# Hybrid decoder step on one core: page numbers read ahead, a logits buffer for each prompt tile, output weights in two places, unread products in two pauses

## The reference

```python
def layer_step(x, pos, lp, attn, ...):
    cols = x @ lp['w_in']
    ...                                   # rotary, indexer keys
    y_a = attn(q, k, v, qi, ki, wi)       # top-k attention, 4 heads of 64
    y_b, ... = rwkv7_mix(...)             # recurrence with a matrix state
    y_c, ... = gated_short_conv(...)
    y_d, ... = rglru_block(...)
    mix = jnp.concatenate([y_a, y_b, y_c, y_d], axis=-1) @ lp['w_out']
    x = layer_norm(DEEPNORM_ALPHA * x + mix, lp['ln1_g'], lp['ln1_b'])
    ffn = moe(x, w_router, router_bias, ...)      # 16 experts, 2 for each row
    x = layer_norm(DEEPNORM_ALPHA * x + ffn, lp['ln2_g'], lp['ln2_b'])

# in attention, for the keys selected by the indexer
logits = jnp.einsum('bthd,btkhd->bthk', q, k_sel) * A_HEAD_DIM ** -0.5
logits = jnp.where(valid[:, :, None, :], logits, -jnp.inf)
p = jax.nn.softmax(logits, axis=-1)
return jnp.einsum('bthk,btkhd->bthd', p, v_sel)
```

## Time and profile before

| | us |
|---|---|
| median of 3 runs (1496.24 to 1502.35) | 1501.76 |
| profiled execution | 1498.81 |
| its span | 1497.2 |
| TensorE busy in the span | 1235.8 |
| VectorE / ScalarE / GpSimd busy | 662.0 / 345.4 / 160.3 |

### The profile page before, as it was taken

How to read it: one execution, slowest core, us unless ns; L and a number is a source line. 1 busy time by engine, 2 the same in 40 slices (tenths; PEclk the granted TensorE clock), 3 DMA queues, 4 the chain that set the end, 5 groups by cost and what they waited for, 6 DMA issues and landing times.

```text
span 1497.2 us, 22283 instructions
## 1 busy us (share of the span) xinstructions
PE 1235.8 (83%) x8296; PEld 777.7 (52%) x8296; DVE 662.0 (44%) x1379; ACT 345.4 (23%) x798; POOL 160.3 (11%) x224
## 2 busy tenths in 40 slices
PE   4989999985899099999398899998679944999950
PEld 2566778952445044444156677897344532444420
DVE  0036898876144301111453469997632350111118
ACT  1044241204222011111143423320322210111110
POOL 0040007003000200000201000430310002000011
PEclk9988999986799599999699799998789966999985
DMA  6095210016442469997512021100538005999943
GB/s 255 7 380 231 71 57 19 4 49 183 182 198 94 180 237 365 355 368 264 192 69 64 15 70 57 42 8 3 150 115 345 1 28 218 332 367 368 358 152 128
DMA packets 67917, 246.30 MB, mean 165 GB/s; under 512 B 8722, under 2 KB 29362, under 8 KB 58674
## 3 DMA queue, kind: packets, MB, share of 16 engines
q1 hardware_dynamic: 48736, 177.17, 32.9%
q0 software_dynamic: 14048, 50.00, 9.4%
q10 hardware_dynamic: 5042, 17.90, 2.9%
HBM read 194.39 MB, written 52.87 MB: 165 GB/s over the span
## 4 chain that ended last, share of the span: by engine, by line
PE 73%; DVE 10%; ACT 4%; DMA 3%; issue 3%; SPq 3%; DVEq 2%; POOL 1%; POOLq 0%; ACTq 0%
PE ps L1227 15%; PE ps L694 12%; PE ps L827 10%; PE ps L1245 8%; PE ps L1190 8%; PE ps L674 7%; PE ps L1218 2%; SPq L446 1%; PE ps L753 1%; PE ps L1062 1%; DMA arena<-in_wa 1%; POOL rows_in L613 1%; ACT arena L1298 1%; SPq L443 1%; DVE arena L1840 1%
## 5 line engine op out<-in xcount | busy, mean ns | idle before, releaser
L1298 ACT ACTIVATE arena<-ps 128x512 f32<-128x512 f32 (+14 forms) x358 | 155.5, 470 | 693.8 <-PE ps L694 155.5
L694 PE MATMUL ps<-arena 128*128 128x272 f32 x1088 | 261.1, 400 | 0.0
L694 PEld LDWEIGHTS ps<-arena 128*128 128x128 f32 x1088 | 208.9, 193 | 50.6 <-issue 5.5
L1227 PE MATMUL ps<-arena 128*128 128x512 f32 x512 | 230.1, 602 | 4.8 <-ACT arena L1298 4.8
L1227 PEld LDWEIGHTS ps<-arena 128*128 128x128 f32 x512 | 98.3, 193 | 130.1 <-issue 130.1
L827 PE MATMUL ps<-arena 64*64 64x64 f32 (+3 forms) x4016 | 153.1, 236 | 12.5 <-DVE arena L2057 10.3
L827 PEld LDWEIGHTS ps<-arena 64*64 64x64 f32 x4016 | 138.5, 137 | 26.3 <-issue 14.7
L674 PE MATMUL ps<-arena 128*128 128x512 f32 (+1 forms) x256 | 105.6, 573 | 22.5 <-DMA arena<-in_wa 19.0
L1245 PE MATMUL ps<-arena 128*128 128x512 f32 x256 | 117.7, 602 | 3.8 <-DVE arena L2513 3.8
L1190 PE MATMUL ps<-arena 128*128 128x512 f32 x256 | 114.1, 601 | 0.0
L2513 DVE COPY arena<-ps 128x256 f32<-128x256 f32 x32 | 13.6, 426 | 188.1 <-PE ps L1234 188.1
(11 more groups left out here) (344 smaller groups left out, 1322.5 us busy)
## 6 DMA issues: line engine op xcount, KB each, us to landing
arena<-in_w_gu SPq DMA_DIRECT2D x32, 2048.0 KB, 9.9
arena<-in_w_dn SPq DMA_DIRECT2D x32, 1024.0 KB, 9.2
arena<-in_wf SPq DMA_DIRECT2D x34, 512.0 KB, 3.7
arena<-rows_in SPq DMA_DIRECT2D x32, 512.0 KB, 9.6
rows_out<-arena ACTq DMA_DIRECT2D x32, 512.0 KB, 8.4
rows_in<-arena POOLq DMA_DIRECT2D x12, 1024.0 KB, 24.2
arena<-in_cache_v POOLq DMA_DIRECT2D x64, 128.0 KB, 2.7
arena<-in_cache_k SPq DMA_DIRECT2D x64, 128.0 KB, 2.7
```

The lines of the kernel that those rows point to most:

```text
L694: mm = pe.matmul(ps[:, 2 + 2 * h + n % 2, 0:HALF], m.wf[n % 3][:, c, :], m.xT[:, c, h * HALF:h * HALF + HALF], start=c == 0, stop=c == KC - 1)
L1227: mm = pe.matmul(ps[:, 3 + k, :], m.xgT[:, c, :], m.w_gu[k][:, c, :], start=c == 0, stop=c == KC - 1)
L1298: return act.activation(out, in_, ACT.Copy)
```

## The change

Five things are edited.

1. The page numbers are read into 32 registers on SyncE and on GpSimd ahead of the wait for the recurrence; the loops over the pages are written out.
2. `m.lg` gets four buffers, one for each tile, two of them in LN0; the maxima and sums get four places too. The wait on `pt_mm` in `masked` goes. The lists of TensorE, ScalarE and VectorE are put in another order: logits(2) ahead of output(0), logits(3) ahead of output(1), the sample's logits ahead of output(2); three maskings before the first scaling; the sample's exponentials ahead of tile 3's copies.
3. The output weights are loaded in two halves, into R2 (after the sample's first logits half) and R1 (after tile 2's values). Expert 0's weights, which also lie in R2, are loaded after the projection's last product instead of at the end of attention.
4. The scatters of tiles 0 to 2 and of tiles 3 and 4 are counted in two semaphores.
5. `warm(n)` puts n products of 128x512 into a PSUM bank that nobody reads: 6 after the first of these semaphores, 5 after the first gathered rows of layer 0's last norm.

```diff
-    m.lg, m.pT = [view(R1, 4, 384), view(R1 + 4096, 4, PAST)], [view(R1 + 6144, 4, 384), view(R1 + 1536, 4, PAST)]
+    m.lg = [view(at, 4, P * (i + 1)) for i, at in enumerate((LN0 + DM, LN0, R1, R1 + 4096))]
+    m.pT = [view(R1 + 1536, 4, 384), view(R1 + 6144, 4, PAST)]
...
+        def page_of(b):
+            return sp.value_load(pages[0:1, b:b + 1], min_val=0, max_val=NPHYS - 1)
+
+        ahead = [page_of(b) for b in range(32)]
         sp.wait_ge(s["rw_mm"], nth(l, "rw_mm", len(RW_PE)))
...
-        for g in range(2):
-            with sp.Fori(0, 4) as j:
-                for c in range(NPAGE):
-                    page = sp.value_load(pages[0:1, bass.ds(j * NPAGE + (16 * g + c), 1)], min_val=0, max_val=NPHYS - 1)
-                    if g and c == 0:
-                        sp.wait_ge(s["state_out"], nth(l, "state_out", 64))
-                    sp.dma_start(m.K[g][:, :, bass.ds(j, 1), PAGE * c:PAGE * c + PAGE],
...
-        sp.wait_ge(s["pv_mm"], nth(l, "pv_mm", 4))
-        sp.dma_start(m.wout, layer_of(din["wout"], l)).then_inc(s["wout_in"], 16)
+        for b in range(2 * 4 * NPAGE):
+            g, j, c = b // (4 * NPAGE), b // NPAGE % 4, b % NPAGE
+            page = ahead[b] if b < len(ahead) else page_of(b)
+            if b == 4 * NPAGE:
+                sp.wait_ge(s["state_out"], nth(l, "state_out", 64))
+            sp.dma_start(m.K[g][:, :, j:j + 1, PAGE * c:PAGE * c + PAGE],
...
+        sp.wait_ge(s["s_lg_mm"], nth(l, "s_lg_mm", 1))
+        sp.dma_start(m.wout[0], layer_of(din["wout"], l)[:, 0:KC // 2, :]).then_inc(s["wout_in"], 16)
+        sp.wait_ge(s["pv_mm"], nth(l, "pv_mm", 3))
+        sp.dma_start(m.wout[1], layer_of(din["wout"], l)[:, KC // 2:KC, :]).then_inc(s["wout_in"], 16)
...
-        for k in range(2):
-            up_weights(k, k)
-            down_weights(k, k)
+        up_weights(1, 1)
+        down_weights(1, 1)
+        sp.wait_ge(s["mix_mm"], nth(l, "mix_mm", 5))
+        up_weights(0, 0)
+        down_weights(0, 0)
...
-        sp.wait_ge(s["x_scattered"], nth(l, "x_scattered", 160))
+        sp.wait_ge(s["x_scattered"], nth(l, "x_scattered", 96))
+        sp.wait_ge(s["x_spread"], nth(l, "x_spread", 64))
...
+    def warm(n):
+
+        for _ in range(n):
+            pe.matmul(ps[:, 7, :], ident, m.consts[:, 0:512], start=True, stop=True)
...
+        pe.wait_ge(s["yg0_in"], nth(l - 1, "yg0_in", 32))
+        warm(5)
         transposes_of_x(l - 1, 5, 0, 0)
...
         y_gates(l, (6, 6), slice(SEQ, T))
+        logits(2)
         pe.wait_ge(s["yn_std"], nth(l, "yn_std", 1))
         output(0)
-        logits(2)
+        logits(3)
         output(1)
-        logits(3)
+        sample_logits(l)
         output(2)
-        sample_logits(l)
         output(3)
...
         mm.then_inc(s["slots_mm"], 1)
+        pe.wait_ge(s["x_scattered"], nth(l, "x_scattered", 96))
+        warm(6)
...
         y_norm(l)
-        exps(0)
-        for i in range(NT):
-            if i + 1 < NT:
-                exps(i + 1)
-            else:
-                for g in range(2):
-                    act.wait_ge(s["s_lg_mm"], nth(l, "s_lg_mm", g + 1))
-                    copy(m.s_lg[g][:, 0:PAST], ps[:, 2 - 2 * g, :])
-                    copy(m.s_lg[g][:, PAST:T], ps[:, 3 - 2 * g, 0:NS]).then_inc(s["s_lg"], 1)
-            turned(i)
-            output(i)
-
+        for i in range(3):
+            exps(i)
+        turned(0)
+        output(0)
+        turned(1)
+        output(1)
+        exps(3)
+        for g in range(2):
+            act.wait_ge(s["s_lg_mm"], nth(l, "s_lg_mm", g + 1))
+            copy(m.s_lg[g][:, 0:PAST], ps[:, 2 - 2 * g, :])
+            copy(m.s_lg[g][:, PAST:T], ps[:, 3 - 2 * g, 0:NS]).then_inc(s["s_lg"], 1)
+        turned(2)
+        output(2)
         for g in range(2):
             act.wait_ge(s["s_max"], nth(l, "s_max", g + 1))
             act.activation(m.s_lg[g], m.s_lg[g], ACT.Exp, bias=m.nmax[g][:, 0:1], accum_out=m.ssum[g][:, 0:1])\
                 .then_inc(s["s_exp"], 1)
+        turned(3)
+        output(3)
...
             dve.wait_ge(s["lg_mm"], nth(l, "lg_mm", i + 1))
-            if i >= 2:
-                dve.wait_ge(s["pt_mm"], nth(l, "pt_mm", 4 * (i - 1)))
...
         y_centred(l)
-        masked(0)
-        masked(1)
-        normed(0)
+        for i in range(3):
+            masked(i)
+        for i in range(3):
+            normed(i)
+        masked(3)
         y_rates(l, 0)
-        normed(1)
-        masked(2)
+        normed(3)
         y_rates(l, 1)
-        normed(2)
-        masked(3)
-        y_scaled(l)
-        normed(3)
         for g in range(2):
             dve.wait_ge(s["s_lg"], nth(l, "s_lg", g + 1))
             dve.tensor_reduce(m.nmax[g][:, 0:1], m.s_lg[g], AX.X, ALU.max, negate=True).then_inc(s["s_max"], 1)
+        y_scaled(l)
         y_out(l)
```

More of the change, by code:

```diff
@@ L238, in memory @@
     st = view(SM0, 680)
-    m.nmax, m.ssum, m.rsum = ([st[:, 8 * k + 4 * j:8 * k + 4 * j + 4] for j in range(2)] for k in range(3))
+    m.nmax, m.ssum, m.rsum = ([st[:, a + 8 * k + 4 * j:a + 8 * k + 4 * j + 4] for a in (0, 536) for j in range(2)]
+                              for k in range(3))
     m.lam = [st[:, 24 + 2 * k:26 + 2 * k] for k in range(8)]
@@ L250, in memory @@
     m.rest = view(SM0 + 680, 7)
-    m.wa, m.wout = view(R1, KC, ACOLS), view(R1, KC, DM)
+    m.wa, m.wout = view(R1, KC, ACOLS), [view(at, KC // 2, DM) for at in (R2, R1)]
     m.Z = view(R1, 7, TP)
@@ L591, in pool_program, with page_of @@
         pool.dma_start(layer_of(dout["small"], l), m.smalls).then_inc(s["small_out"], 16)
+        def page_of(b):
+            return pool.value_load(m.pages[0:1, b:b + 1], min_val=0, max_val=NPHYS - 1)
+        ahead = [page_of(b) for b in range(32)]
         pool.wait_ge(s["rw_mm"], nth(l, "rw_mm", len(RW_PE)))
@@ L597, in pool_program @@
         pool.drain()
-        for g in range(2):
-            with pool.Fori(0, 4) as j:
-                for c in range(NPAGE):
-                    page = pool.value_load(m.pages[0:1, bass.ds(j * NPAGE + (16 * g + c), 1)], min_val=0, max_val=NPHYS - 1)
-                    pool.dma_start(m.V[g][:, bass.ds(j, 1), c, :],
-                                   din["cache_v"][bass.ds(l * NPHYS + page, 1)].rearrange("z k f -> k z f"))\
-                        .then_inc((s["v0_in"], s["v1_in"])[g], 16)
+        for b in range(2 * 4 * NPAGE):
+            g, j, c = b // (4 * NPAGE), b // NPAGE % 4, b % NPAGE
+            page = ahead[b] if b < len(ahead) else page_of(b)
+            pool.dma_start(m.V[g][:, j:j + 1, c, :], din["cache_v"][bass.ds(l * NPHYS + page, 1)].rearrange("z k f -> k z f"))\
+                .then_inc((s["v0_in"], s["v1_in"])[g], 16)
         pool.wait_ge(s["zeros_out"], ZEROED)
@@ L1173, in output_projection @@
     def output_projection(l):
-        pe.wait_ge(s["wout_in"], nth(l, "wout_in", 16))
+        pe.wait_ge(s["wout_in"], nth(l, "wout_in", 32))
         pe.wait_ge(s["attn_done"], nth(l, "attn_done", 1))
@@ L1538, in exps @@
             for h in range(4):
-                x = m.lg[i % 2][:, h, 0:P * (i + 1)]
-                ins = act.activation(x, x, ACT.Exp, bias=m.nmax[i % 2][:, h:h + 1], accum_out=m.ssum[i % 2][:, h:h + 1])
+                x = m.lg[i][:, h, :]
+                ins = act.activation(x, x, ACT.Exp, bias=m.nmax[i][:, h:h + 1], accum_out=m.ssum[i][:, h:h + 1])
             ins.then_inc(s["p_exp"], 1)
@@ L2500, in experts @@
         dispatch(l)
-        dve.wait_ge(s["x_scattered"], nth(l, "x_scattered", 160))
+        dve.wait_ge(s["x_scattered"], nth(l, "x_scattered", 96))
+        dve.wait_ge(s["x_spread"], nth(l, "x_spread", 64))
         dve.wait_ge(s["xt_mm"], nth(l, "xt_mm", 5))
```

28 lines of the change are left out of this document (14 added, 14 removed).

## The result

The changed kernel takes 1445.36 us, the median of its runs (1444.28 to 1449.53), beside 1499.0 for the kernel before (1495.32 to 1502.35): a ratio of 0.9656 (95% interval 0.9636 to 0.9676), 3.4% faster. The profiled execution took 1444.28 us, its span is 1442.4.

A forecast was written before the change was run, and what follows sets the result against it. TensorE bounds nearly everywhere, so only stretches where it waits, chiefly in attention, can shorten. From 1498.81 us, attention's 35.7 (17.6 + 18.1) came off and all else was booked 0, giving 1463; range of 8 in 10: 1448 to 1482.

The forecast's parts named there:

- What bounds the kernel: Whole kernel: TensorE nearly everywhere, so only stretches where it waits can shorten; in attention it is busy 55.5 of 80.2 us.
- Part 1, attention: Attention: a logits buffer for each tile and the new order cut it to 62.6 us, saving 17.6 + 18.1 = 35.7 us.
- The clock worked out for layer 0: Layer 0's attention followed through the new order: output(0) ends at 348.8, output(3) at 378.0, attention at 389.4.
- the last, from the sample's transposes to the projection: End of attention: 11.4 us taken, between layer 1's 12.71 and 10.0 at the high clock throughout.
- Output projection: Stage behind attention, to its last transposes: no change forecast, 0 us.
- Part 2, pages: Key pages in attention: reading numbers ahead makes a page about 0.8 us, last seen near 361; booked 0, range 0 to +7 a layer.
- The slower rival: Attention: pages still cost 1.51 us, so the sample's second half holds up outputs 2 and 3; some 1504 us, chance 0.05.
- The prediction's dividing line: Key pages in attention: the slower case decides from a page cost of 1.4 us.
- Part 3: Output weights loaded in two halves during attention: both there by 380, 9 us early; price 0, at worst 3 us a layer.
- Part 4, the products: Unread products before the first experts and in the norm pause: done 2.6 us before the transposes, clock falls again; 0 taken.
- the warm clock holds: Pauses with unread products: TensorE enters transposes and first products at 2.4 GHz; price -8 us, 1455, chance 0.10.
- a change of more than 4 us outside attention: Sign of being wrong: the stretches outside attention change by more than 4 us.

The follow-up runs named there:

- the last run: Changed kernel with three more unread products in the norm pause and the third column product moved before the second three head transposes: 1442.97 us, ratio 0.9644.

## Why the prediction was wrong, step by step

**What bounds the kernel** was read rightly: 40.6 of the 54.8 us came from the idle stage that it named, and the experts, where TensorE is full, kept their length to 0.1 us.

**Part 1, attention: 40.6 instead of 35.7.** The clock worked out for layer 0 holds until the end of output(3), within a microsecond: output(0) ends at 348.7 (said 348.8), logits(3) at 352.4 (352.7), output(1) at 356.4 (357.2), the sample's halves at 360.3 and 364.4 (361.0, 364.8), output(3) at 377.1 (378.0). The low clock for logits(3) fits the changed kernel (3.78 and 3.79 us), and that is partly luck: in layer 0 the six other kernels with this order took 2.88 to 2.94 us for them. The term that was mis-sized is the last, from the sample's transposes to the projection: 10.0 us was named as the high-clock length, 11.4 was taken, and 10.03 came (377.11 to 387.14). That and the 0.9 before it make 2.3 in layer 0; layer 1 gave 2.6.

**Output projection: -4.1 where nothing was booked.** The prediction took the pause of 2.07 us as idle time and saw that the sample's products behind it were slow. It didn't follow the slow clock past the stage's end. In before it reached into layer 0's projection (6.07 us in all for the first product, 2.4 more than the 3.66 after); with the pause gone TensorE enters it at the high clock. Layer 1 is another matter: it entered at the high clock before too. Its 1.7 us are one block of 16 instructions (8.81 us at a granted clock of 0.81, against 7.11) in the middle of a stretch in which TensorE never waits. The first product and this block before, and the block after:

```profile
406.95 6.07 PE L1179 MATMUL ps<-arena 128*32 128x256 f32 x64 [0.94 <-issue]
...
1185.88 8.81 PE L1190 MATMUL ps<-arena 128*128 128x512 f32 x16
...
1137.88 7.11 PE L1210 MATMUL ps<-arena 128*128 128x512 f32 x16
```

The same block was slow in the run with the looped pages (both layers) and in that with the products alone (layer 1), and in no kernel with the new order and the pages ahead. But the run with the pages alone has the old order, and there it took 7.11 us in both layers. What slows it wasn't found, so these 1.7 us can't be put down to the change. The 1.6 us of layer 1's projections and recurrence came with the new order each time (299.7 to 299.9 us, against 300.5 to 301.5 with the old one; the last run changes the stage itself); their cause wasn't looked for.

**Part 2, pages: right, and closer to the edge than the median shows.** The page cost is 0.91 us ((28.84 - 0.54) / 31, the last issue taken off), between the 0.8 and the 0.93 given for full engines, and the last page is seen at 360.55, said 361. The reads are covered: SyncE's wait at that point fell from 82.9 to 63.9 us. In every kernel with the pages ahead and the new order, layer 0's last page is there 34.3 to 34.4 us after the last update's start (33.6 in one). TensorE asks for it after 34.2 us in the changed kernel, where logits(3) ran at the low clock, and after 33.2 where they ran faster. Then it waits 1.0 to 1.2 us, the clock falls, and the half costs 3.3 to 3.5 us instead of 1.95: the attention with the faster logits is the longer one, 62.5 in the kernel without products against 61.0. In the one kernel whose page came at 33.6 the wait was 0.35 us and layer 0's attention took 60.2. The Trainium skill ("DMA: Bandwidth & Descriptors", "Issuing engines are not separate DMA queues") says that starting transfers from several engines saves only the sequencer's time, which is usually small beside the transfer. Here it was not small: with the loops SyncE set the pace at 1.51 us a page and a share of 0.63. With the numbers read ahead the engines set it, at 0.97, though an issue still takes 0.54 of the 0.91 us.

The slower rival is the case that the run with the loops made: 1.51 us a page, a wait of 20 us before the sample's second half. Its estimate of 1504 was for the products worth nothing; with their 5 us off (1492.15 beside 1497.38) it comes to 1499, and 1497.09 was measured. The prediction's dividing line was a page cost of 1.4 us. The runs have two points, 0.91 us with 3.4% gained and 1.51 us with nothing gained; where between them the gain ends wasn't measured.

**Part 3: 0 is right, and its cover is needed.** The prediction named the cover as 9 us; taken away with the old load point, it cost some 10 us in two layers.

**Part 4, the products: -8.2 where 0 was taken.** This is the step that failed. The prediction took 0.86 us a product at the low clock, "twice 6.88/16". But 6.88 us is the time of 16 instructions, and the code makes eight products there: each is two instructions in this trace. So a product takes 0.86 at the high clock already and twice that at the low one; six of them take 7.57 with the clock rising on the way, and reach the rows instead of ending 2.6 us before. Of the 8.2 us in the pauses the run without them gives back 6.5. Of the rest 1.4 lies in layer 1's first expert, which was slow in the trace of the kernel before; in the run with the pages alone, which has no unread products either, it took 13.76 us instead of 15.42. Its products in these two traces:

```profile
1255.65 10.16 PE L1227 MATMUL ps<-arena 128*128 128x512 f32 x16 [1.21 <-ACT arena L1298]
...
1254.95 8.51 PE L1232 MATMUL ps<-arena 128*128 128x512 f32 x16 [1.21 <-ACT arena L1303]
```

The expected fall of the clock in such a gap is real, as the run with half of the products shows. The rival "the warm clock holds" gave -8 and had a chance of 0.10; its size was right by luck and its reason not: no clock held through a gap, there was none, and the 8.2 us came as 2.8, 4.7 and 0.7, not as three times 2.7. For the norm pause the prediction's argument was right, with ScalarE's 3.45 us as the gap, and 0.7 was all that was gained there. The Trainium skill ("TensorE: Matmul & The Clock Gate", Part 1) says that the low clock is the default and that activity releases it. That was on the side of these products, and the trace agrees as far as they reach the work: the granted clock from 502.58 to 504 is 1.00. The prediction had named a change of more than 4 us outside attention as a sign of being wrong; it came to 14.2.

**The range.** The end of attention, layer 0's projection and the pauses erred in the same direction, because all three hang on the clock. The range treated them as separate, and its low end took in only a part of one. The products alone would have left the time inside it (1463 - 8.2 = 1455); with attention's 4.9 us and the projection's 4.1 it fell below.

## What to carry to other kernels

Price an idle gap on TensorE as its own length plus the slower clock of what follows, up to the next stretch of sustained work, and look for that second part beyond the stage in which the gap lies. Count it only where TensorE sets the pace: in attention a faster clock only lengthened the next wait. When an order is changed so that something is asked for earlier, put the time at which it is asked for beside the time at which it can be there: here either edit alone was worth nothing. A row counts instructions: before a price for one call is taken from it, ask how many instructions a call makes. And place filler so that it ends at the arrival of what it fills for.

## What the runs showed of the hardware

A wait of a microsecond can cost more than itself. Before a half of the sample's logits, with the same 16 instructions behind it, waits of 0.23, 0.30 and 0.35 us left 1.95 us, and waits of 1.01, 1.15 and 1.20 us were followed by 3.28, 3.42 and 3.52 us; in the first of these the granted clock from 360.42 to 363.70 was 0.57. The kernel before has such a wait in layer 1, and it is shorter:

```profile
1107.96 3.51 PE L1111 MATMUL ps<-arena 128*32 128x512 f32 x16 [0.59 <-DMA arena<-in_cache_k]
```

Not every wait of this length does it. In the changed kernel 1.21 us before the first expert's products left the granted clock at 1.00 (504.89 to 512.01), and with more products 0.87 us before the row projection did (716.69 to 723.70). What decides between the two wasn't measured.

While the pages came in, all transfers together moved 276 GB/s at a share of 0.97 (330 to 361, above); behind the single load of the output weights they moved 400 GB/s at 1.01 (391.56 to 398.08). So the pages meet the engines' bound at fewer bytes.
